# Attention projections of a two-block transformer kernel: three products of split operands in place of one float32 product

## The chip, the cores and the metric

The kernel runs on one core of a Trainium2 chip. The metric is the device time of one launch in microseconds (us), as the median of repeated runs. TensorE (PE, with its weight loads as PEld), VectorE (DVE), ScalarE (ACT), GpSimd (POOL) and SyncE (SP, which here only issues DMAs) run their own instruction streams and meet at semaphores.

## The reference, cut to what matters

Two transformer blocks run one after the other. The change is in the first one's mixer, attention with a forget gate, over 1024 tokens of width 1024 with 16 heads of 64 columns:

```python
def fox_mixer(x, w_in, b_f, w_out):
    proj = x @ w_in                      # [1024, 3 * 1024 + 16]
    q, k, v, f_logit = jnp.split(proj, [D_MODEL, 2 * D_MODEL, 3 * D_MODEL], axis=-1)
    ...
    log_f = jax.nn.log_sigmoid(f_logit.astype(jnp.float32) + b_f)
    c = jnp.cumsum(log_f, axis=1).transpose(0, 2, 1)
    ...
    s = jnp.einsum('bhqd,bhkd->bhqk', qi, k) * scale + cqi[..., None] - c[:, :, None, :]
    s = jnp.where(kpos[None, :] <= qpos[:, None], s, -jnp.inf)
    pr = jax.nn.softmax(s, axis=-1)
    o = jnp.einsum('bhqk,bhkd->bhqd', pr, v)
    return o @ w_out
```

Layer norm, a gated feed-forward network, and a second block (retention, a gated delta rule, a mixture of experts) follow. They are untouched.

## The kernel before, in words

**Stages.** The first stage is `stage_attention` (L127). The output projection, the FFN and the second block follow, each stage a block of its own that starts when the one before has ended.

**Pairs and units.** The attention stage works on pairs of heads (8 pairs p of 128 columns) and in each on 8 units t, one per 128 query rows; u = 8p + t. A unit t has t + 1 key blocks for each of the two heads. On PE a unit is, in this order (the loop after L357): `scores(u)`, `weigh(u-2)` (probabilities times v), one piece of projection work, `turn_first(u-1)` (128x128 transposes of the probabilities, the first 8), a second piece, `turn_second(u-1)` (the other transposes), the remaining pieces. In units 3 and 7 both first pieces stand ahead of `turn_first`. DVE does the row maxima, the output copy of u-2, the normalisation of both heads and the copies of the first transposes (`row_max`, `output`, `normalize`, `turned_copy`, L384 to L414). ACT does both exponentials, then the copies of finished pieces (`fill_copy`, L468) and of the second transposes (`turned_copy`, L500), in that order; in units 0 and 4 the copies of pieces come last.

**The projections.** q, k and v of a pair are made in six groups of four pieces (`V_LOW, Q_HIGH, K_HIGH, V_HIGH, Q_LOW, K_LOW`, L123), spread over the units by `PIECE_FROM` (L124); `LOW` and `HIGH` are the two halves of the tokens, `Q_LOW` and `K_LOW` are already for the next pair. All groups use the same PSUM bank 7: the first piece of a group waits until ACT has copied out the group before (`fill_out`). A q or k piece is two products of 128x128 weights (stationary) with 128x512 of x transposed (moving), in float32. A v piece is eight products of 128x128 of x with 128x128 of weights, in float32, and gives v with the tokens on the partitions. In the trace each float32 product is two MATMUL records. `scores(u)` of a wide unit waits for the exponentials of u-1, and from t = 4 on for the copy of K_HIGH.

**The weights.** `wqk` and `wv` are double buffered; SP loads a pair's weights once the products that read the buffer have ended (L233 to L241), two pairs ahead, and then loads the output projection's weights. GpSimd does nothing in the stage but issue one DMA.

**The start.** The first pair's q and k (both halves) are made up front in banks 0 to 3, k chunk by k chunk (L343 on). After chunk 3 PE does the forget gate's 64 thin products (f_bank), after chunk 5 one product that carries the sums over the tiles (L357). DVE makes the gate's cumulative sum in three bfloat16 parts (to L447), and SP spreads these with 24 small DMAs (L230). The first `scores` waits for all 24.

## Time and profile before

| | us |
|---|---|
| median of three runs | 3608.33 (3604.4 to 3608.97) |
| the profiled execution's own time | 3608.7 |
| its span on the core | 3606.9 |
| PE busy | 3174.3 (88%), 14928 matmul records |
| DVE, ACT, POOL busy | 1521.3 (42%), 1085.0 (30%), 1054.8 (29%) |

The span is what lies between the first and the last instruction of the core. Busy time is a union of instructions; a matmul's record is longer than the time to the next one's start, since matmuls overlap in the array. The rate of PE is therefore read from start to start. The granted clock is a share of full speed (1.00 is 2.4 GHz, 0.50 is 1.2 GHz).

### The profile page before, as it was taken

What the parts mean: (1) busy time and instruction counts of PE and PEld (TensorE: products, weight loads), DVE (VectorE), ACT (ScalarE), POOL (GpSimd) and SP (SyncE); (2) the same over time, 40 slices, a digit from 0 to 9 for tenths busy, and PEclk for the clock granted to TensorE, in tenths of its full rate; (3) what the DMA queues carried; (4) which work ended last, traced back from release to release, by engine and by line L of the source; (5) the groups of instructions that cost most, each with busy time, mean ns of one, the idle gap of its engine ahead of it and who ended that gap; (6) DMA issues with size and microseconds to landing.
All of it is one profiled execution on the core that took longest, in us unless ns stands there. A gap on an engine that the chain in (4) does not pass through costs nothing. (4 is left out here: it accounts for less than half of the span.)

```text
span 3606.9 us, 40987 instructions
## 1 busy us (share of the span) xinstructions
PE 3174.3 (88%) x14928; PEld 2220.4 (62%) x14928; DVE 1521.3 (42%) x2003; ACT 1085.0 (30%) x1457; POOL 1054.8 (29%) x539
## 2 busy tenths in 40 slices
PE   7999999979999979949699897999595799999993
PEld 4656566448888868834344444999542577777772
DVE  2443444431111111145520334444513778787875
ACT  1222222111111112210120122222202477777773
POOL 0000000123333324420000212222000378787774
PEclk9999999989999989969899998999797799999996
DMA  2000010211111132225510103100123699999995
GB/s 106 18 18 19 18 65 1 82 47 47 47 47 47 47 116 93 99 116 175 188 48 0 40 30 121 73 13 1 47 83 120 216 364 372 368 369 370 370 372 217
DMA packets 115216, 450.08 MB, mean 125 GB/s; under 512 B 14481, under 2 KB 15441, under 8 KB 109089
## 3 DMA queue, kind: packets, MB, share of 16 engines
q1 hardware_dynamic: 102066, 401.03, 30.1%
q0 software_dynamic: 7856, 28.64, 2.4%
q10 hardware_dynamic: 5184, 18.88, 1.3%
q8 instruction: 77, 1.26, 0.1%
q14 instruction: 33, 0.27, 0.0%
HBM read 404.30 MB, written 44.10 MB: 124 GB/s over the span
## 5 line engine op out<-in xcount | busy, mean ns | idle before, releaser
L2601 DVE TENSOR_TENSOR moe_w_low<-moe_raw_up,moe_w_high 128x1024 fp32r<-128x1024 f32 x288 | 436.4, 1553 | 156.5 <-ACT moe_w_high L2541 156.5
L2464 POOL TENSOR_TENSOR moe_w_low<-moe_raw_down,moe_w_high 128x1024 fp32r<-128x1024 f32 x144 | 417.3, 2928 | 148.4 <-ACT moe_w_high L2551 148.4
L2541 ACT ACTIVATE moe_w_high<-moe_raw_up 128x1024 fp32r<-128x1024 f32 x288 | 304.6, 1061 | 188.1 <-PE ps L2504 110.4
L91 PE MATMUL ps<-x1T_high,w_up_high 128*128 128x512 f32 x704 | 278.7, 396 | 13.7 <-POOL w_up_low L737 13.7
L91 PE MATMUL ps<-x1T_low,w_up_high 128*128 128x512 f32 x704 | 281.8, 400 | 0.0
L91 PE MATMUL ps<-x1T_high,w_up_low 128*128 128x512 f32 x704 | 276.9, 393 | 0.0
L585 POOL TENSOR_TENSOR res<-res,ln_b 128x1024 f32<-128x1024 f32 x16 | 37.5, 2346 | 780.3 <-DVE res L577 780.3
L253 PE MATMUL ps<-x0T,wqk 128*128 128x512 f32 x512 | 241.7, 608 | 10.3 <-DMA x0T<-in_xT 8.5
L2519 PE MATMUL ps<-moe_w_high,moe_x_high 128*128 128x512 f32 x576 | 229.4, 398 | 4.2 <-DVE moe_x_low L2632 4.2
L2521 PE MATMUL ps<-moe_w_high,moe_x_low 128*128 128x512 f32 x576 | 225.9, 392 | 0.0
L2520 PE MATMUL ps<-moe_w_low,moe_x_high 128*128 128x512 f32 x576 | 225.8, 392 | 0.0
L391 DVE TENSOR_REDUCE top<-ps 128x1 f32<-128x256 f32 (+7 forms) x128 | 91.0, 753 | 262.8 <-PE ps L298 262.8
L735 POOL TENSOR_TENSOR w_up_high<-w_up,consts 128x1024 fp32r<-128x1024 f32 x44 | 83.4, 1896 | 300.7 <-PE ps L91 289.3
L80 PE MATMUL ps<-xT,w_cols 128*128 128x512 f32 x384 | 171.2, 599 | 0.0
L497 ACT ACTIVATE probs<-ps,top 128x256 f32<-128x256 f32 (+7 forms) x128 | 93.9, 738 | 255.3 <-DVE top L391 255.3
L80 PE MATMUL ps<-w_rows,xT 128*128 128x512 f32 x384 | 165.5, 593 | 0.0
L91 PEld LDWEIGHTS ps<-x1T_high,w_up_high 128*128 128x128 f32 x704 | 132.8, 189 | 48.6 <-POOL w_up_low L737 14.1
L91 PE MATMUL ps<-w_down_high,h_high 128*128 128x512 f32 x352 | 137.8, 391 | 23.9 <-POOL w_down_low L873 22.6
L2551 ACT ACTIVATE moe_w_high<-moe_raw_down 128x1024 fp32r<-128x1024 f32 x144 | 147.2, 1055 | 35.2 <-DVE xT L2621 25.8
L873 POOL TENSOR_TENSOR w_down_low<-w_down,w_down_high 128x1024 fp32r<-128x1024 f32 x44 | 105.7, 2403 | 170.6 <-ACT w_down_high L857 170.6
L2504 PE MATMUL ps<-moe_w_high,moe_hid_high 128*128 128x512 f32 x288 | 101.5, 434 | 60.4 <-POOL moe_w_low L2464 60.4
L253 PEld LDWEIGHTS ps<-x0T,wqk 128*128 128x128 f32 x512 | 91.0, 191 | 101.8 <-issue 98.1
(417 smaller groups left out, 5918.4 us busy)
## 6 DMA issues: line engine op xcount, KB each, us to landing
moe_raw_up<-in_w SPq DMA_DIRECT2D x288, 512.0 KB, 10.3
moe_raw_down<-in_w SPq DMA_DIRECT2D x144, 512.0 KB, 7.3
w_ada<-in_w_ada SPq DMA_DIRECT2D x48, 512.0 KB, 4.7
w_up<-in_ffn_w_up SPq DMA_DIRECT2D x22, 1024.0 KB, 4.8
w_down<-in_ffn_w_down SPq DMA_DIRECT2D x44, 512.0 KB, 3.4
y_rows<-xT ACTq DMA_DIRECT2D x36, 512.0 KB, 8.2
wqk<-in_attn_wqk SPq DMA_DIRECT2D x8, 1024.0 KB, 4.9
y_rows<-zero_rows SPq DMA_DIRECT2D x1, 8192.0 KB, 29.2
```

The source lines that it names most:

```text
L80: ins = pe.matmul(out, stationary, moving, start=(n == 0), stop=(n == last))
L91: ins = pe.matmul(out, stationary, moving, start=start and n == 0, stop=stop and n == last)
L253: return pe.matmul(ps[:, bank, :], wqk[:, p % 2, k, j * P:(j + 1) * P], m.xT[:, k, h * HALF:(h + 1) * HALF], start=(k == 0), stop=(k == DT ...
L873: pool.tensor_tensor(w_low[:, s], w[:, s], w_high[:, s].bitcast(F32), ALU.subtract).then_inc(w_split[s], 1)
L2464: pool.tensor_tensor(w_low[:, down_slot(k)], raw_down[:, k], w_high[:, down_slot(k)].bitcast(F32), ALU.subtract).then_inc(down_low, 1)
L2504: ins = pe.matmul(ps[:, 5 + n, :], h[:, k, :], w[:, n * HALF:(n + 1) * HALF], start=first, stop=last)
L2519: pe.matmul(ps[:, 2 + j, :], x_high[:, k, :], high, start=first and a == 0, stop=False)
L2520: pe.matmul(ps[:, 2 + j, :], x_high[:, k, :], low, start=False, stop=False)
L2521: ins = pe.matmul(ps[:, 2 + j, :], x_low[:, k, :], high, start=False, stop=last and a == 1)
L2541: act.activation(w_high[:, up_slot(n)], raw_up[:, n], ACT.Copy).then_inc(up_high, 1)
L2551: act.activation(w_high[:, down_slot(k)], raw_down[:, k], ACT.Copy).then_inc(down_high, 1)
L2601: dve.tensor_tensor(w_low[:, up_slot(n)], raw_up[:, n], w_high[:, up_slot(n)].bitcast(F32), ALU.subtract).then_inc(up_low, 1)
```

## The change

x transposed and each pair's weights are split in a high part, which ACT writes as float32r (a Copy), and a low part, the difference, also float32r. Each product becomes three matmuls: high by high, high weights by low x, low weights by high x. v is made like q and k, with the weights stationary: its 128x512 result is v transposed. ACT copies it to `vT`, and a new piece of four 128x128 transposes (`VT_LOW`, `VT_HIGH`), which ACT copies out again, turns it. So there are eight groups of 4, 1, 4, 4, 4, 1, 4, 4 pieces. A q, k or v piece is now 6 matmuls of 128x512; a VT piece is 4 transposes. The units get 4, 4, 3, 2, 4, 4, 3, 2 pieces (before: 4, 3, 3, 2, 4, 3, 3, 2).

Weights are kept in three slots (v, q, k), raised by ACT at the end of units 3 (q), 4 (k) and 6 (v) for the next pair and lowered by GpSimd. One raw buffer serves all three: SP loads the next tensor when GpSimd has lowered the one before. At the start the first pair's q weights and all of x are lowered by DVE, its k and v weights by GpSimd. The thin products use the raw x. The product with the carries moves from after chunk 5 to after chunk 6. The output projection's weights are loaded after the last pair's V_HIGH, as their place holds the low x until then. The 24 spreading DMAs come in another order. The diff, cut:

```diff
-PIECES = 4
-V_LOW, Q_HIGH, K_HIGH, V_HIGH, Q_LOW, K_LOW = range(6)
-PIECE_FROM = (0, 4, 7, 10, 12, 16, 19, 22, 24)
+V_LOW, VT_LOW, Q_HIGH, K_HIGH, V_HIGH, VT_HIGH, Q_LOW, K_LOW = range(8)
+GROUP_SIZE = (4, 1, 4, 4, 4, 1, 4, 4)
+GROUP_AT = (0,) + tuple(itertools.accumulate(GROUP_SIZE))
+PIECE_GROUP = [g for g, n in enumerate(GROUP_SIZE) for _ in range(n)]
+PIECE_FROM = (0, 4, 8, 11, 13, 17, 21, 24, 26)
+V, Q, K = range(3)
...
-        wqk = sb("wqk", [P, 2, DT, 2 * P])
-        wv = sb("wv", [P, 2, DT, P])
-        wf = sb("wf", [P, DT, THIN])
+        x_high, x_low = sb("x0T_high", [P, DT, T], F32R), m.x_low
+        w_raw = sb("qkv_raw", [P, DT, P])
+        w_high, w_low = sb("qkv_high", [P, 3, DT, P], F32R), sb("qkv_low", [P, 3, DT, P], F32R)
+        vT = sb("vT", [P, HALF])
...
+        x_raw = [probs[:, k // 2, k % 2, :] for k in range(4)]
+        x_raw += [probsT[:, k // 2, 8 * (k % 2):8 * (k % 2) + 8, :].rearrange("p k n -> p (k n)") for k in range(4)]
+        first_raw = [None, v[:, 0], v[:, 1]]
+        wf = vT[:, 0:DT * THIN].rearrange("p (k n) -> p k n", n=THIN)
...
+        def wait_slot_free(eng, s, of):
+
+            if s == V:
+                eng.wait_ge(filled, through(of - 1, V_HIGH))
+            elif of == 1:
+                eng.wait_ge(qk_bank, 4)
+            else:
+                eng.wait_ge(filled, through(of - 1, Q_HIGH if s == Q else K_HIGH))
...
+            sp.dma_start(first_raw[Q], d["attn_w"][0, Q]).then_inc(first_loaded[Q], 16)
+            sp.dma_start(x_raw[0], d["xT"][:, 0, :]).then_inc(x_loaded[0], 16)
+            sp.dma_start(first_raw[K], d["attn_w"][0, K]).then_inc(first_loaded[K], 16)
+            for k in range(1, DT):
+                sp.dma_start(x_raw[k], d["xT"][:, k, :]).then_inc(x_loaded[k], 16)
             sp.dma_start(wf[:], d["attn_wf"]).then_inc(f_loaded, 16)
-            sp.dma_start(wqk[:, 0], d["attn_wqk"][0]).then_inc(wqk_loaded[0], 16)
-            for k in range(DT):
-                sp.dma_start(m.xT[:, k, :], d["xT"][:, k, :]).then_inc(x_loaded[k], 16)
             sp.dma_start(bf[:], d["attn_bf"]).then_inc(f_loaded, 16)
-            sp.dma_start(carries[:], d["fg_carries"]).then_inc(f_loaded, 16)
-            sp.dma_start(wv[:, 0], d["attn_wv"][0]).then_inc(wv_loaded[0], 16)
-            sp.dma_start(wqk[:, 1], d["attn_wqk"][1]).then_inc(wqk_loaded[1], 16)
-            sp.dma_start(wv[:, 1], d["attn_wv"][1]).then_inc(wv_loaded[1], 16)
+            sp.dma_start(carries, d["fg_carries"]).then_inc(f_loaded, 16)
+            sp.dma_start(w_raw[:], d["attn_w"][0, V]).then_inc(w_loaded, 16)
...
+            for p in range(1, PAIRS):
+                for s, before in ((Q, V), (K, Q), (V, K)):
+
+                    sp.wait_ge(lowered[before], p + (s != Q))
+                    sp.dma_start(w_raw[:], d["attn_w"][p, s]).then_inc(w_loaded, 16)
+
+            sp.wait_ge(filled, through(PAIRS - 1, V_HIGH))
...
+            def lower(s, of, raw):
+                pool.wait_ge(raised[s], of + 1)
+                pool.tensor_tensor(w_low[:, s], raw, w_high[:, s].bitcast(F32), ALU.subtract
+                                   ).then_inc(lowered[s], 1)
+
+            lower(K, 0, first_raw[K])
+            lower(V, 0, w_raw[:])
+            for p in range(1, PAIRS):
+                for s in (Q, K, V):
+                    lower(s, p, w_raw[:])
...
-            def qk_product(p, j, h, k, bank):
-                return pe.matmul(ps[:, bank, :], wqk[:, p % 2, k, j * P:(j + 1) * P],
-                                 m.xT[:, k, h * HALF:(h + 1) * HALF], start=(k == 0), stop=(k == DT - 1))
+            def product(s, h, k, bank):
+
+                cols = slice(h * HALF, (h + 1) * HALF)
+                pe.matmul(ps[:, bank, :], w_high[:, s, k, :], x_high[:, k, cols], start=(k == 0), stop=False)
+                pe.matmul(ps[:, bank, :], w_high[:, s, k, :], x_low[:, k, cols], start=False, stop=False)
+                return pe.matmul(ps[:, bank, :], w_low[:, s, k, :], x_high[:, k, cols], start=False,
+                                 stop=(k == DT - 1))
             def piece(u, n):
-                p, g, quarter = u // TT, n // PIECES, n % PIECES
-                if quarter == 0:
+                p, g = u // TT, PIECE_GROUP[n]
+                part = n - GROUP_AT[g]
+                if part == 0:
                     pe.wait_ge(fill_out, through(p, g) - 1)
-                if g in (V_LOW, V_HIGH):
-                    t = 4 * (g == V_HIGH) + quarter
-                    pe.wait_ge(wv_loaded[p % 2], 16 * (p // 2 + 1))
-                    ins = group(pe, ps[:, 7, quarter * P:(quarter + 1) * P],
-                                [(m.xT[:, k, t * P:(t + 1) * P], wv[:, p % 2, k, :]) for k in range(DT)])
+                if g in (VT_LOW, VT_HIGH):
+                    for i in range(4):
+                        ins = pe.transpose(ps[:, 7, i * P:(i + 1) * P], vT[:, i * P:(i + 1) * P], m.ident[:])
                 else:
-                    of, j, h = qk_of(p, g)
-                    pe.wait_ge(wqk_loaded[of % 2], 16 * (of // 2 + 1))
-                    for k in (2 * quarter, 2 * quarter + 1):
-                        ins = qk_product(of, j, h, k, 7)
-                if quarter == PIECES - 1:
+                    of, j, h = (p, -1, int(g == V_HIGH)) if g in (V_LOW, V_HIGH) else qk_of(p, g)
+                    pe.wait_ge(lowered[1 + j], of + 1)
+                    for k in (2 * part, 2 * part + 1):
+                        ins = product(1 + j, h, k, 7)
+                if part == GROUP_SIZE[g] - 1:
...
-            pe.wait_ge(wqk_loaded[0], 16)
+            pe.wait_ge(lowered[Q], 1)
             for k in range(DT):
-                pe.wait_ge(x_loaded[k], 16)
+                pe.wait_ge(x_lowered, k + 1)
                 for g in range(4):
-                    ins = qk_product(0, g % 2, g // 2, k, g)
+                    if g == 1:
+                        pe.wait_ge(lowered[K], 1)
+                    ins = product(1 + g % 2, g // 2, k, g)
                     if k == DT - 1:
                         ins.then_inc(qk_bank, 1)
                 if k == 3:
                     pe.wait_ge(f_loaded, 48)
-                    for n in range(4, DT):
+                    for n in range(DT):
                         pe.wait_ge(x_loaded[n], 16)
-                    thin_group(pe, ps[:, 7, 0:FCHUNK], wf, m.xT, TILES).then_inc(f_bank, 1)
-                if k == 5:
+                    for n in range(DT):
+                        for c in range(TILES):
+                            ins = pe.matmul(ps[c * THIN:(c + 1) * THIN, 7, 0:FCHUNK], wf[:, n, :],
+                                            x_raw[n][:, c * FCHUNK:(c + 1) * FCHUNK],
+                                            start=(n == 0), stop=(n == DT - 1))
+                    ins.then_inc(f_bank, 1)
+                if k == 6:
...
+            dve.wait_ge(raised[Q], 1)
+            dve.tensor_tensor(w_low[:, Q], first_raw[Q], w_high[:, Q].bitcast(F32), ALU.subtract
+                              ).then_inc(lowered[Q], 1)
+            for k in range(DT):
+                dve.wait_ge(x_raised, k + 1)
+                dve.tensor_tensor(x_low[:, k, :], x_raw[k], x_high[:, k, :].bitcast(F32), ALU.subtract
+                                  ).then_inc(x_lowered, 1)
...
+                    act.activation(vT[:], ps[:, 7, :], ACT.Copy).then_inc(fill_out, 1)
+                elif g in (VT_LOW, VT_HIGH):
+                    t = 4 * (g == VT_HIGH)
...
+            def raise_weights(s, of):
+                act.wait_ge(w_loaded, 16 * (raw_order(s, of) + 1))
+                if of:
+                    wait_slot_free(act, s, of)
+                act.activation(w_high[:, s], w_raw[:], ACT.Copy).then_inc(raised[s], 1)
+
+            def raise_first(s):
+                act.wait_ge(first_loaded[s], 16)
+                act.activation(w_high[:, s], first_raw[s], ACT.Copy).then_inc(raised[s], 1)
+
+            raise_first(Q)
+            for k in range(DT):
+                act.wait_ge(x_loaded[k], 16)
+                act.activation(x_high[:, k, :], x_raw[k], ACT.Copy).then_inc(x_raised, 1)
+                if k == 0:
+                    raise_first(K)
+            raise_weights(V, 0)
...
+                if p + 1 < PAIRS and t in (3, 4, 6):
+                    raise_weights({3: Q, 4: K, 6: V}[t], p + 1)
...
+        with ExitStack() as s2:
+            m.x_low = sb(s2, "x0T_low", [P, DT, T], F32R)
```

## Rows read from the trace of the kernel before

**Rows 1.** Busy time by stretch: engines, then PE clock, DMA share.

```profile
core 0: us, PE busy (x) PEld busy (x) DVE busy (x) ACT busy (x) POOL busy (x), PEclk, DMA share, GB/s
...
42.00:55.00 13.00, 0.11 (x1) 0.00 (x0) 0.00 (x0) 1.88 (x2) 0.00 (x0) 0.67 0.03 6
55.00:60.00 5.00, 4.80 (x25) 4.49 (x26) 1.29 (x6) 0.81 (x4) 0.00 (x0) 0.50 0.58 210
...
85.00:358.00 273.00, 270.76 (x1775) 168.08 (x1775) 113.18 (x246) 68.61 (x157) 0.00 (x0) 1.00 0.06 20
...
630.00:640.00 10.00, 8.43 (x60) 3.98 (x60) 5.75 (x12) 3.02 (x6) 0.00 (x0) 1.00 0.01 2
```

**Rows 2.** Timeline of SyncE's queue, issues in two neighbouring pairs.

```profile
227.23 0.33 SPq L238 DMA_DIRECT2D wqk<-in_attn_wqk  x1
...
304.10 0.33 SPq L238 DMA_DIRECT2D wqk<-in_attn_wqk  x1
```

**Rows 3.** Timeline of one pair, TensorE: start us, us, line, tiles.

```profile
371.42 3.70 PE L253 MATMUL ps<-x0T,wqk 128*128 128x512 f32 x8 [0.25 <-ACT qk L465]
...
386.49 1.04 PE L308 MATMUL ps<-consts,probs 128*128 128x128 f32 x8
387.37 5.52 PE L80 MATMUL ps<-wv,x0T 128*128 128x128 f32 x48
392.82 1.13 PE L291 MATMUL ps<-qk 64*128 64x512 f32 x4
...
396.29 1.98 PE L253 MATMUL ps<-x0T,wqk 128*128 128x512 f32 x4
...
406.69 1.98 PE L253 MATMUL ps<-x0T,wqk 128*128 128x512 f32 x4
```

**Rows 4.** Timeline of the start, all engines.

```profile
7.72 0.23 DVE L420 CAST ident<-consts 128x128 bf16<-128x128 f32 x1 [7.72 <-DMA consts<-in_consts]
...
8.54 15.82 PE L253 MATMUL ps<-x0T,wqk 128*128 128x512 f32 x32 [8.54 <-DMA x0T<-in_xT]
...
27.89 7.13 PE L253 MATMUL ps<-x0T,wqk 128*128 128x512 f32 x16
...
34.86 0.28 PE L357 MATMUL ps<-within,fg_carries 128*128 128x1 f32 x2
...
37.54 16.48 SPq L230 DMA_DIRECT2D negc<-parts  x24
...
55.20 0.80 PE L291 MATMUL ps<-qk 64*128 64x128 f32 x4 [13.09 <-DMA negc<-parts]
```

**Rows 5.** Timeline, TensorE in the FFN, first and last of 57 matmuls.

```profile
819.77 0.40 PE L91 MATMUL ps<-x1T_low,w_up_high 128*128 128x512 f32 x1
...
832.84 0.39 PE L91 MATMUL ps<-x1T_high,w_up_high 128*128 128x512 f32 x1
```

**Rows 6.** Timeline of the pair of rows 3, ScalarE.

```profile
370.77 0.60 ACT L465 ACTIVATE qk<-ps 128x512 f32<-128x512 f32 x1 [0.46 <-PE ps L253]
...
398.04 0.20 ACT L497 ACTIVATION_READ_ACCUMULATOR probs<-ps,top 128x1 f32 x1
...
408.71 0.60 ACT L465 ACTIVATE qk<-ps 128x512 f32<-128x512 f32 x1
```

**Rows 7.** Page, costliest groups: raising and lowering 128x1024 tiles elsewhere.

```profile
L2601 DVE TENSOR_TENSOR moe_w_low<-moe_raw_up,moe_w_high 128x1024 fp32r<-128x1024 f32 x288 | 436.4, 1553 | 156.5 <-ACT moe_w_high L2541 156.5
...
L2541 ACT ACTIVATE moe_w_high<-moe_raw_up 128x1024 fp32r<-128x1024 f32 x288 | 304.6, 1061 | 188.1 <-PE ps L2504 110.4
...
L873 POOL TENSOR_TENSOR w_down_low<-w_down,w_down_high 128x1024 fp32r<-128x1024 f32 x44 | 105.7, 2403 | 170.6 <-ACT w_down_high L857 170.6
```

**Rows 8.** DMA issues, 0 to 700 us: size, time to landing.

```profile
w_attn_out<-in_attn_w_out SPq DMA_DIRECT2D x2, 2048.0 KB, 10.3
```

**Rows 9.** Groups by form, 60 to 660 us: the widest normalisation.

```profile
L402 DVE TENSOR_SCALAR probs<-probs,inv 128x1024 f32<-128x1024 f32 x16 | 12.1, 754 | 0.6
```

**Rows 10.** Timeline of the last pair, TensorE, a unit without pieces.

```profile
636.44 0.66 PE L308 MATMUL ps<-consts,probs 128*128 128x128 f32 x4 [1.57 <-DVE probsT L411]
```

More of the change, by code:

```diff
@@ L203, in pieces @@
             p, t = u // TT, u % TT
-            return [n for n in range(PIECE_FROM[t], PIECE_FROM[t + 1]) if not skipped(p, n // PIECES)]
+            return [n for n in range(PIECE_FROM[t], PIECE_FROM[t + 1]) if not skipped(p, PIECE_GROUP[n])]
         def through(p, g):
-            return 6 * p + g + 1 - 2 * (p > 0 or g > K_HIGH)
+            return 8 * p + g + 1 - 2 * (p > 0 or g > K_HIGH)
         def qk_of(p, g):
@@ L328, in weigh @@
                 p, t = u // TT, u % TT
-                pe.wait_ge(fill_out, through(p, V_HIGH if t >= 4 else V_LOW))
+                pe.wait_ge(fill_out, through(p, VT_HIGH if t >= 4 else VT_LOW))
                 pe.wait_ge(first_out, firsts[u + 1])
@@ L351, in _ @@
                     pe.wait_ge(f_loaded, 48)
-                    for n in range(4, DT):
+                    for n in range(DT):
                         pe.wait_ge(x_loaded[n], 16)
-                    thin_group(pe, ps[:, 7, 0:FCHUNK], wf, m.xT, TILES).then_inc(f_bank, 1)
-                if k == 5:
+                    for n in range(DT):
+                        for c in range(TILES):
+                            ins = pe.matmul(ps[c * THIN:(c + 1) * THIN, 7, 0:FCHUNK], wf[:, n, :],
[3 more added lines that the diff above has]
+                if k == 6:
                     pe.wait_ge(f_step, 5)
-                    pe.matmul(ps[:, 6, 0:1], carries[:], within[:, FCHUNK - 1:FCHUNK], start=True, stop=True
+                    pe.matmul(ps[:, 6, 0:1], carries, within[:, FCHUNK - 1:FCHUNK], start=True, stop=True
                               ).then_inc(carried, 1)
@@ L517, in _ @@
             for u in range(UNITS):
-                ends = [n for n in pieces(u) if n % PIECES == PIECES - 1]
+                p, t = u // TT, u % TT
+                ends = [n for n in pieces(u) if n + 1 in GROUP_AT]
                 late = u % TT in (0, 4)
```

74 lines of the change are left out of this document (32 added, 42 removed).

## The prediction

> **What bounds the kernel now.** I first read the busy time by stretch, to see what the attention stage waits for. Over the middle pairs PE is busy 270.76 of 273 us at clock 1.00, DVE 113.18, ACT 68.61 and POOL 0 [rows 1]: PE is the bound and three engines have room. The DMA queue's timeline gives the length of a pair, 304.10 - 227.23 = 76.87 us [rows 2]. The timeline of PE through a pair shows hardly a hole; the one short wait is 0.25 us, for ACT's copy out of bank 7 [rows 3]. So time that PE saves in a pair is saved in the end, as far as what the pieces cover (row maxima, exponentials, copies) does not come out from under them. The start is another regime: PE stands idle about 13 us until the spreading DMAs of the gate have landed, and the chain to them is carries product at 34.86, issues from 37.54, scores at 55.20 [rows 4]. There, only what moves the carries product counts.
>
> **The products.** A float32 q or k group is 8 products of 512 columns. 16 records took 27.89 to 34.86, 6.97 us [rows 4]; I leave some 0.1 of it to the change-over at the end, which stays, so 6.87. The new matmul exists elsewhere, in the FFN: 57 starts from 819.77 to 832.84 are 0.2334 us apart, with a weight load for each and the clock full [rows 5]. A group of 24 costs 5.60, so a q or k group saves 1.27. A v group is 64 records; 48 of them took 387.37 to 392.82, 5.45 us [rows 3], so 7.27 in all; against 5.60 it saves 1.67. The new turning piece has four transposes; eight took 386.49 to 387.37, 0.11 each [rows 3], so it costs 0.44. Per middle pair, then: 4 x 1.27 + 2 x 1.67 - 2 x 0.44 = 7.5 us.
>
> **The new waits.** The turning piece is a group of its own in the one bank 7. The next piece waits until ACT has copied it out, and ACT does its exponentials first, so ahead of that copy a whole row maximum and exponential stand. I follow each unit with the times of rows 3 and 6.
> - Unit 5: the projection work starts at 396.29. Four transposes to 396.73, `turn_first` (8 x 0.11) to 397.61. ACT's last exponential ends at 398.04 + 0.20 = 398.24 [rows 6], the copy takes 0.60, PE sees it 0.05 later, as it does after the copy at 370.77 (end 371.37, PE at 371.42 [rows 3, 6]): 398.89. The wait is 1.3; the change-over of 0.1 is in it: 1.2. Queued behind it on PE are three q pieces, `turn_second` and the scores of unit 6; DVE and ACT wait for those.
> - Unit 6: piece at 406.69, now 1.40 and a change-over to 408.19, `turn_first` to 409.07. ACT's copy can't start before 408.71, as now [rows 6], and ends at 409.31: PE goes on at 409.36. Wait 0.3. It is hidden now, by the longer piece.
> - Unit 1: exponentials are short there. The transposes drain for about 0.17 (a record of 1.04 is followed by the next start after 0.88 [rows 3]), the copy is 0.60, the wake-up 0.05, and two transposes of 0.22 cover: 0.6. I take 0.5.
> - Unit 2's wait of 0.25 stays: piece and copy move up together. The other boundaries have a whole `scores` and `weigh` between them.
> Together 2.0 per pair, so a middle pair saves 7.5 - 2.0 = 5.5 us and lasts 71.3.
>
> **The pairs in sum.** Six middle pairs: 33.0. Pair 0 has two v groups and the next pair's two q/k groups: 3.3 + 2.5 - 0.44 (the other turning piece stands in a stretch that waits for the softmax chain) - 1.5 for units 5 and 6 = 3.9. Pair 7: 3.3 + 2.5 - 0.44 - 0.5 = 4.9; its units 5 to 7 have no pieces and already wait for DVE 1.57 us [rows 10], which covers the turning piece. Sum 41.8.
>
> **Raising and lowering.** Per pair ACT gets 3 raisings of 1.06 [rows 7] and 2 more copies of 0.60, 4.4 us on an engine busy a quarter of the time; they are queued after a unit's last copy, and the next exponential waits for a `scores` and a row maximum, over 3 us in the wide units, so I cost them at nothing; without that cover at 1.06 each, 22 us. The second path is raise, lower (POOL, 2.40 [rows 7]), load 0.5 MB. The load is under the 10.3 us that 2 MB took [rows 8]. Three rounds of under 14 us fit in 71. Q is raised at the end of unit 3 and used in unit 5, K at 4 and 6, v at 6 and in the next pair: a unit of some 9 us (71.3 / 8) lies between. On SP the loads stand behind the 24 spreading DMAs once, and behind nothing later. The output projection's weights now start at the end of the last pair's unit 4, with three units and the tail of the stage left; at 76.87 / 8 = 9.6 us a unit, less without pieces, that is over 20 us as an estimate, and two overlapping loads of 10.3 [rows 8] fit.
>
> Does the lowering hold up DVE? The widest normalisation takes 754 ns for 1024 elements, while a subtraction of two tiles as wide takes 1553 on the same engine [rows 7, 9], so DVE has a fast form for it. The Trainium skill (SBUF — State Buffer, Who interferes with whom) says that such a form, or one with two SBUF inputs, and a GpSimd operation shut each other out for a whole instruction; no row of this stage has both. By place there is no meeting: q's lowering would run about 1.1 to 3.5 us into unit 4, k's 1.8 to 4.2 into unit 5, while unit 5's last exponential ends 398.24 - 392.82 = 5.4 into the unit [rows 3, 6] and the normalisation comes near there. I take nothing in the pairs; the upper end is a rival.
>
> **The start.** PE began at 8.54 [rows 4]. Now DVE must first finish the small casts (from 7.72 [rows 4], some 0.5), then lower q's weights and chunk 0 of x; alone I put each at 1.4 (1.55 where GpSimd works too [rows 7]). So PE starts at about 11.0. Up to the carries product it has 7 chunks of 12 matmuls (19.6), the 3.5 of the thin products (24.36 to 27.89) and some 2 us of half clock, as now (the first 32 records took 15.8 where their later pace gives 13.8 [rows 4]): 36.1. k's weights, 2.4 us on POOL after a raising, are ready about 0.5 later than PE asks for them. If POOL's lowering gets ahead of DVE's chunk 0 it is 2.4 more. Against 34.86 this is 1.8 to 4 us later; I take 2.5. Nothing gains: the spreading and its 24 issues stay, and the first scores with them.
>
> **Sum.** 41.8 - 2.5 = 39.3 us. From the profiled execution, 3608.7 (span 3606.9 and 1.8 around it), that is 3569.4; the median is 0.4 lower, so 3569. Later stages load nothing in other order, and I cost them at zero.
>
> **Rivals.**
> - **The waits stay hidden** (ACT is free earlier than in the old rows, since the scores come sooner after the last copy): 6 x 2.0 + 1.5 + 0.5 = 14 less, 3555. Against: both terms of unit 5's wait are read straight from ACT. Chance 0.09.
> - **The chain comes out further.** The shorter pieces uncover more: the scores waiting for the exponentials, `turn_second` for DVE's copies as in the last pair, or ACT's raisings in front of an exponential. Another 1.5 us per pair in seven pairs: 3580. Chance 0.14.
> - **The clock.** Between 42 and 55 us PE was idle, and the next 5 us had clock 0.50 [rows 1]; but in 630 to 640, with waits of 1.57, it was 1.00 [rows 1, 10]. Were two stretches of 3.5 us in each of seven pairs at half clock, each would cost 1.75: 24.5 us, 3594. The Trainium skill (TensorE: Matmul & The Clock Gate, A second HAM failure mode: psum-queue depth-cycling) has a kernel whose small idle times between groups did this, and the one bank 7 is such a queue. The last pair speaks against. Chance 0.06.
> - **Slower: GpSimd's lowering shuts DVE out.** Place: `normalize` of units 4, 5 and 7, with PE's transposes behind it. If each of 3 x 7 lowerings delays PE by its whole 2.40: 50.4 us, 3620. It passes 3609 once each costs over 39.3 / 21 = 1.9. For it: POOL goes from 0 to 7.2 us per pair. Against: the places above, and that most of DVE's work in a unit reads PSUM. Chance 0.04.
> - **It doesn't do what it says:** the three matmuls are no faster than the one float32 product here (another operand or weight-load limit) and the time is within 7 us of before. Against: the same form at 0.2334 in the FFN. Chance 0.02.
> - The forecast: 0.65, by itself 3560 to 3578 (the start 1.8 to 4, unit 5's wait 0.8 to 2 in seven pairs, the groups' savings 10% off).
>
> **Range and chances.** 3555 to 3584 takes in the first two rivals and leaves out the last three. 0.2% is about 7 us, what a measurement of this kernel can tell from no change. Faster 0.94 (forecast, the first three rivals), same 0.02, slower 0.04.
>
> **What would show it.** In the changed trace: SP issues of neighbouring pairs 71.3 apart; matmuls of `ps<-w_high,x_high` 0.23 apart; PE waiting for ACT's copy of vT's transposes 1.2 us in unit 5 and about 0.5 in unit 1; first `scores` near 57.7; the stage's end some 39 us earlier; DVE's means in the stage as before. The prediction is wrong if PE's clock falls in the stage, if DVE's normalisations get longer, or if ACT stands at a raising for a load.

## The result, and the profile after

| | before | changed |
|---|---|---|
| median, us | 3606.62 (3604.4 to 3608.97, 4 runs) | 3561.06 (3559.79 to 3562.18, 4 runs) |
| profiled execution, span | 3606.9 | 3557.7 |
| first load of the next stage (end of attention) | 653.98 | 613.01 |
| what follows to the end of the span | 2952.9 | 2944.7 |

The ratio is 0.9873, 95% interval 0.9861 to 0.9886. Run again beside other kernels, the same code gave 0.9888 (0.9873 to 0.9903), experiment e11. The forecast was 3569 (3555 to 3584).

Where the time went is read first from the stage's end. These are the first loads of the next stage, in the timeline of SyncE's queue before and after:

```profile
653.98 0.33 SPq L610 DMA_DIRECT2D res<-in_x  x1
```

```profile
613.01 0.33 SPq L680 DMA_DIRECT2D res<-in_x  x1
```

653.98 - 613.01 = 41.0 us; the forecast for the stage was 39.3. The other 8 us between the two profiled spans are behind the stage, where nothing was changed. Over all thirteen profiles of this study (the kernels before and changed, and the eleven experiments, which all share that rest) it took between 2944.7 and 2953.5. One place of this scatter is seen in the timelines of TensorE in the mixing stage, the same 256 records before and after:

```profile
2617.59 113.04 PE L80 MATMUL ps<-qkv,xT 128*128 128x512 f32 x256 [2.80 <-DMA qkv<-in_w_mix_out]
```

```profile
2574.80 110.13 PE L80 MATMUL ps<-qkv,xT 128*128 128x512 f32 x256 [1.87 <-DMA qkv<-in_w_mix_out]
```

They start 42.8 us apart and end 45.7 apart, 2.9 us more: in the 25 us around their start PE's granted clock was 0.77 in the one (2605 to 2630) and 0.92 in the other (2562 to 2587). The other 5 us are not placed. So the two executions that were profiled lie 8 us apart behind the stage, and the 41 us at the stage's end are read as the change; e11 comes back to this.

**Through the pairs.** Busy time by stretch of the changed kernel, beside [rows 1] (columns as there):

```profile
core 0: us, PE busy (x) PEld busy (x) DVE busy (x) ACT busy (x) POOL busy (x), PEclk, DMA share, GB/s
...
42.00:55.00 13.00, 0.00 (x0) 0.00 (x0) 0.00 (x0) 0.00 (x0) 0.00 (x0) 0.57 0.03 6
55.00:60.00 5.00, 3.31 (x13) 2.59 (x14) 1.30 (x6) 0.81 (x4) 0.00 (x0) 0.50 0.34 107
...
85.00:355.00 270.00, 261.46 (x1742) 182.84 (x1738) 118.44 (x263) 85.00 (x184) 26.63 (x11) 1.00 0.07 22
```

PE is now busy 261.46 of 270 us, where it was 270.76 of 273. It has real holes, and the clock stays at 1.00. The timeline of POOL gives the length of a pair, as SP's queue did in [rows 2], since it lowers q's weights once per pair:

```profile
359.85 2.65 POOL L272 TENSOR_TENSOR qkv_low<-qkv_raw,qkv_high 128x1024 fp32r<-128x1024 f32 x1 [39.48 <-ACT qkv_high L564]
...
431.16 2.65 POOL L272 TENSOR_TENSOR qkv_low<-qkv_raw,qkv_high 128x1024 fp32r<-128x1024 f32 x1 [39.51 <-ACT qkv_high L564]
```

71.31 us; before 76.87, forecast 71.3. The holes, in TensorE's timeline of one pair (units 5, 6 and 1), beside [rows 3]:

```profile
371.92 0.66 PE L300 MATMUL ps<-consts,vT 128*128 128x128 f32 x4
372.42 1.04 PE L342 MATMUL ps<-consts,probs 128*128 128x128 f32 x8
374.41 0.50 PE L286 MATMUL ps<-x0T_high,qkv_high 128*128 128x512 f32 x1 [0.96 <-ACT v L527]
...
384.44 1.04 PE L342 MATMUL ps<-consts,probs 128*128 128x128 f32 x8
385.55 0.50 PE L286 MATMUL ps<-x0T_high,qkv_high 128*128 128x512 f32 x1
...
411.61 0.66 PE L300 MATMUL ps<-consts,vT 128*128 128x128 f32 x4
412.10 0.38 PE L342 MATMUL ps<-consts,probs 128*128 128x128 f32 x2
412.95 0.50 PE L286 MATMUL ps<-x0T_high,qkv_high 128*128 128x512 f32 x1 [0.47 <-ACT v L527]
```

The turning piece at 371.92 takes 0.50, `turn_first` at 372.42 follows, and then PE waits 0.96 us for ACT's copy of the turned v (L527). The same in unit 1: 0.47 before 412.95. Before 385.55 there is a hole of 0.24, counted otherwise: at its pace of 0.11 per transpose `turn_first`, from 384.44, would have let the next start at 385.31. Counted so, unit 5's hole is 1.1. ScalarE's timeline of the same units shows why, beside [rows 6]:

```profile
373.68 0.20 ACT L547 ACTIVATION_READ_ACCUMULATOR probs<-ps,top 128x1 f32 x1
373.77 0.59 ACT L527 ACTIVATE v<-ps 128x512 f32<-128x512 f32 x1
...
384.91 0.59 ACT L513 ACTIVATE qk<-ps 128x512 f32<-128x512 f32 x1
...
412.30 0.60 ACT L527 ACTIVATE v<-ps 128x512 f32<-128x512 f32 x1 [1.00 <-PE ps L300]
```

In unit 5 the copy at 373.77 follows the exponential's end directly: ACT was busy, and the piece had long been ready. The same in unit 6 at 384.91, behind an exponential that ends at 384.82 + 0.09. In unit 1, at 412.30, ACT had waited for PE: there the wait is only the copy's own 0.60.

**The start.** TensorE's timeline, beside [rows 4]:

```profile
9.82 0.77 PE L286 MATMUL ps<-x0T_high,qkv_high 128*128 128x512 f32 x1 [9.82 <-DVE x0T_low L469]
...
11.95 0.79 PE L286 MATMUL ps<-x0T_high,qkv_high 128*128 128x512 f32 x1 [0.51 <-POOL qkv_low L272]
...
36.34 0.28 PE L398 MATMUL ps<-qk 128*128 128x1 f32 x2
...
56.69 0.80 PE L325 MATMUL ps<-qk 64*128 64x128 f32 x4 [17.22 <-DMA negc<-parts]
```

PE starts at 9.82 and not at 8.54, has to wait 0.51 for k's low weights from POOL, reaches the carries' product at 36.34 (34.86 before) and the first scores at 56.69 (55.20). So the start costs 1.5 us in this execution.

### The profile page after: what moved, and what is told of

Same layout as the page of the kernel before. It is cut to its first block and busy times, and to the rows that moved or that the text cites. A ratio compares the mean times of both kernels' runs of the same rounds, so it can differ in the third digit from the quotient of the medians.

```text
span 3557.7 us, 40458 instructions
## 1 busy us (share of the span) xinstructions
PE 3116.4 (88%) x14608; PEld 2227.6 (63%) x14608; DVE 1536.4 (43%) x2012; ACT 1124.6 (32%) x1505; POOL 1114.3 (31%) x562
## 5 line engine op out<-in xcount | busy, mean ns | idle before, releaser
L272 POOL TENSOR_TENSOR qkv_low<-qkv_raw,qkv_high 128x1024 fp32r<-128x1024 f32 x22 | 53.5, 2434 | 468.8 <-ACT qkv_high L564 468.8
L286 PE MATMUL ps<-x0T_high,qkv_high 128*128 128x512 f32 x384 | 163.9, 427 | 22.5 <-ACT v L527 10.0
L91 PEld LDWEIGHTS ps<-x1T_high,w_up_high 128*128 128x128 f32 x704 | 132.5, 188 | 45.7 <-POOL w_up_low L807 14.2
L91 PE MATMUL ps<-w_down_high,h_high 128*128 128x512 f32 x352 | 138.1, 392 | 23.8 <-POOL w_down_low L943 22.5
L2621 ACT ACTIVATE moe_w_high<-moe_raw_down 128x1024 fp32r<-128x1024 f32 x144 | 147.2, 1056 | 33.4 <-DVE xT L2691 29.5
L91 PEld LDWEIGHTS ps<-x1T_low,w_up_high 128*128 128x128 f32 x704 | 132.5, 188 | 34.6
```

The lines of the kernel that those rows point to most:

```text
L91: ins = pe.matmul(out, stationary, moving, start=start and n == 0, stop=stop and n == last)
L286: pe.matmul(ps[:, bank, :], w_high[:, s, k, :], x_high[:, k, cols], start=(k == 0), stop=False)
L2621: act.activation(w_high[:, down_slot(k)], raw_down[:, k], ACT.Copy).then_inc(down_high, 1)
```

## The experiments

Lengths of pairs are read from POOL's timeline, as above. Where a run was made once, its verdict is read from the attention stage of its profile; its time in the table has the scatter of the rest. Pairs repeat within 0.1 us, but the stage's end is not that sharp: the changed kernel's own code gave 613.01 and 614.26 (e11). Two places of this scatter show. In the start the first matmuls stand 0.43 apart, and how long they do differs: to 16.4 in the changed kernel, to 14.7 in e4 and e8, to 18.0 in e11. In the stage's last unit the 16 transposes and the waits between them take 2.6 us in nine of the thirteen profiles and 3.3 to 3.6 in e1, e2, e4 and e7, at a granted clock of 0.66 in place of 1.00; so the stages of these four end some 1 us late.

| | pair, us | first scores | stage's end | time, us |
|---|---|---|---|---|
| before | 76.87 | 55.20 | 653.98 | 3606.62 |
| changed | 71.31 | 56.69 | 613.01 | 3561.06 |
| e1 no turning | 68.59 | 57.23 | 595.63 | 3547.13 |
| e2 float32 in the pieces | 79.05 | 56.90 | 670.76 | 3624.54 |
| e3 turned v between | 70.38 | 56.70 | 606.52 | 3560.03 |
| e4 carries after chunk 5 | 71.26 | 53.27 | 611.13 | 3561.51 |
| e5 POOL twice | 71.37 | 56.32 | 612.81 | 3568.47 |
| e6 DVE lowers | 71.32 | 56.37 | 612.44 | 3567.81 |
| e7 two products | 60.96 | 56.97 | 538.25 | 3488.91 |
| e8 early gate | 71.31 | 47.79 | 604.26 | 3555.11 |
| e9 two queues | 71.31 | 50.50 | 606.52 | 3556.3 |
| e10 three parts | 70.43 | 42.28 | 592.26 | 3542.15 |
| e11 changed again | 71.32 | 57.64 | 614.26 | 3565.98 |

### e1: no turning of v

```diff
-GROUP_SIZE = (4, 1, 4, 4, 4, 1, 4, 4)
-PIECE_FROM = (0, 4, 8, 11, 13, 17, 21, 24, 26)
+GROUP_SIZE = (4, 4, 4, 4, 4, 4)
+PIECE_FROM = (0, 4, 7, 10, 12, 16, 19, 22, 24)
...
                 if g in (V_LOW, V_HIGH):
-                    act.activation(vT[:], ps[:, 7, :], ACT.Copy).then_inc(fill_out, 1)
-                elif g in (VT_LOW, VT_HIGH):
-                    t = 4 * (g == VT_HIGH)
+                    t = 4 * (g == V_HIGH)
                     act.activation(v[:, p % 2, t:t + 4, :]..., ps[:, 7, :], ACT.Copy).then_inc(fill_out, 1)
```

> Leaves out the turning of v: the two turning groups and their copies are gone, the schedule of units is the one of before, and v is copied out as it is (transposed, so the result is another). Theory (turning costs its transposes plus the waits for ACT's copy): per middle pair 2 x 0.49 for the transposes, 0.96 in unit 5 and 0.47 in unit 1, together 2.4 us; neighbouring pairs 68.9 us apart where the changed kernel has 71.3, and about 18 us less in all, 3543. Rival (the waits are only moved: the softmax chain then shows at the same places): 1 us per pair, 3553.

POOL's timeline:

```profile
418.14 2.65 POOL L272 TENSOR_TENSOR qkv_low<-qkv_raw,qkv_high 128x1024 fp32r<-128x1024 f32 x1 [38.40 <-ACT qkv_high L559]
...
486.73 2.65 POOL L272 TENSOR_TENSOR qkv_low<-qkv_raw,qkv_high 128x1024 fp32r<-128x1024 f32 x1 [38.39 <-ACT qkv_high L559]
```

68.59 us per pair, 2.72 less than the changed kernel (2.4 expected); the stage ends 17.4 us sooner (some 18.5 but for the slow last unit); the ratio to the kernel before is 0.9841 (0.9823 to 0.9859). No wait for the copy of v is left in its waits. So turning v costs its transposes and its two waits, 2.4 us by the rows above, and 0.3 more that I put down to the change-overs around them without a row for it; the softmax chain did not take its place.

### e2: one float32 product in the pieces

```diff
-                        ins = product(1 + j, h, k, 7)
+                        ins = pe.matmul(ps[:, 7, :], w_high[:, 1 + j, k, :].bitcast(F32),
+                                        x_high[:, k, h * HALF:(h + 1) * HALF].bitcast(F32),
+                                        start=(k == 0), stop=(k == DT - 1))
```

> The pieces of q, k and v use one float32 product of the high parts in place of the three float32r matmuls (the low parts are left out there); the start, raising, lowering, turning and all waits stay as in the changed kernel. Theory (PE bound; what the split saves is the products): a group goes from 24 x 0.23 = 5.5 to 6.87 us, six groups per pair give 8.2, less the 0.25 wait of unit 6 that is covered again: pairs 79.2 us apart, the stage about 61 us longer than the changed kernel's, 3622, above the kernel before by what turning, its waits and the start cost. Rival (the gain comes from v being made like q and k, not from the three products): under 30 us longer.

TensorE's timeline:

```profile
386.90 3.70 PE L305 MATMUL ps<-x0T_high,qkv_high 128*128 128x512 f32 x8
390.44 0.82 PE L344 MATMUL ps<-consts,probs 128*128 128x128 f32 x6
...
408.17 1.98 PE L305 MATMUL ps<-x0T_high,qkv_high 128*128 128x512 f32 x4 [0.96 <-ACT v L529]
...
450.42 5.42 PE L305 MATMUL ps<-x0T_high,qkv_high 128*128 128x512 f32 x12 [0.47 <-ACT v L529]
```

A pair takes 79.05 (79.2 expected), the stage is 57.7 us longer than the changed one's: 6 x 7.74 = 46.4 in the middle pairs, the rest in the first and the last, which have four groups each and not six. 61 were expected, with 1.37 us per group. Two pieces take 386.90 to 390.44, 3.54 us, against 2.87 in the changed kernel, so a group saves 1.34, and six of them less the 0.24 of unit 6, which the longer piece covers here, give the 7.74 to 0.1. The waits of units 5 and 1 are where they were, 0.96 and 0.47, though the pieces are longer: no piece stands ahead of them. Against the kernel before this one is slower, ratio 1.0063 (1.0042 to 1.0084), 16.8 us at the stage's end. That is the price of the new structure without its product: turning (17.4 by e1) and the start (1.5), less what v gains by 512 columns in one product; that difference, 2 us as it stands and nearly 5 without the slow last unit of e1 and e2, is read from no row of its own.

### e3: the turned v between the exponentials

```diff
                 exponent(u, 0)
+                if t == 5:
+                    fill_copy(u, ends[0])
+                    ends = ends[1:]
                 exponent(u, 1)
```

> In unit 5 ACT copies the turned v between its two exponentials, not behind them. Theory (PE's wait of 0.96 in unit 5 is ACT's order): the wait falls to about 0.1, pairs 70.4 us apart, the stage 7 us shorter. Rival (the second exponential, 0.6 later, delays the next scores or DVE's normalisation and gives it back): pairs stay at 71.3.

The waits, 60 to 614 us (us in total, times, longest):

```profile
PE ps L286 <- ACT v L527: 3.3, 7, 0.5
```

Pairs of 70.38, as expected, and the stage ends 6.5 us sooner. Of PE's waits for the copy of v, 10.0 us in 14 times, 3.3 in 7 remain: unit 1's. The wait of unit 5 was ACT's order of work. Its single time, 3560.03, shows nothing of this, 6.5 us being inside the scatter of a single run.

### e7: two products

```diff
-                        ins = product(1 + j, h, k, 7)
+                        pe.matmul(ps[:, 7, :], w_high[:, 1 + j, k, :], x_high[:, k, cols], start=(k == 0),
+                                  stop=False)
+                        ins = pe.matmul(ps[:, 7, :], w_low[:, 1 + j, k, :], x_high[:, k, cols], start=False,
+                                        stop=(k == DT - 1))
```

> Leaves out the middle product (high weights by low x) in the pieces, so a piece is 4 matmuls. Theory (PE is still the bound after the change, but its cover is thin): a group costs 3.7 in place of 5.5, 6 x 1.85 = 11.1 us per pair if nothing came out from under it; the waits for ACT's copies and DVE's turned tiles grow in units 2, 5, 6 and 7 by some 0.4 each, so pairs at about 62. Rival (the softmax chain is already next): pairs over 66.

The waits, 60 to 614 us (us in total, times, longest):

```profile
PE ps L306 <- ACT v L531: 10.0, 14, 1.0
...
PE ps L306 <- ACT qk L517: 7.0, 14, 0.5
```

60.96 per pair, where about 62 were expected: 10.35 less, of 11.1 at most. The waits for copies of v are unchanged and those for copies of q and k went from 1.8 to 7.0 us over the stage. The chain of maxima and exponentials is not the next bound: another third of the products could go and nine tenths of it would come out at the end.

### e5 and e6: GpSimd twice, and DVE in its place

```diff
                 pool.wait_ge(raised[s], of + 1)
+                if of:
+                    pool.tensor_tensor(spare[:], raw, w_high[:, s].bitcast(F32), ALU.subtract)
```

> GpSimd does each lowering of the pairs from the second on twice, the first time into a spare tile. Theory (GpSimd is covered and its places miss DVE's normalisations, apart from short overlaps): POOL's work doubles to 14 us per pair, DVE's normalisations grow by at most one overlap per pair (about 1 us, not on PE's path), pairs stay at 71.3 us. Rival (GpSimd shuts DVE out and PE pays): pairs get several us longer.

DVE's and POOL's timelines around unit 4:

```profile
362.80 2.07 DVE L446 TENSOR_SCALAR probs<-probs,inv 128x640 f32<-128x640 f32 x1
364.78 1.27 DVE L455 COPY probsT<-ps 128x512 f32<-128x512 f32 x2
```

```profile
359.50 2.65 POOL L274 TENSOR_TENSOR spare<-qkv_raw,qkv_high 128x1024 fp32r<-128x1024 f32 x1 [37.15 <-ACT qkv_high L567]
362.12 2.39 POOL L275 TENSOR_TENSOR qkv_low<-qkv_raw,qkv_high 128x1024 fp32r<-128x1024 f32 x1
```

This is the lock in plain view: a normalisation of 640 columns, 554 ns otherwise, starts at 362.80 and takes 2.07 us; POOL's second lowering starts at 362.12 and takes 2.39, to 364.51. It ends at 364.87, 0.36 behind the lowering, so part of its own 0.55 was done under it. The mean of this form over the stage is 1131 ns, that of 768 columns 1247 in place of 621: 2.8 us more of normalisation per pair, where at most 1 was expected. The pair nevertheless takes 71.37. What stands behind the normalisation, the copies of turned tiles, is needed by PE only later: its waits for them are 7.0 us in 11 times over the stage, as in the changed kernel. So one half of the rival was right, GpSimd and DVE do shut each other out, and the other half wrong, PE did not pay.

```diff
                 normalize(u, 1)
+                if p + 1 < PAIRS and t in (4, 5, 7):
+                    s = {4: Q, 5: K, 7: V}[t]
+                    dve.wait_ge(raised[s], p + 2)
+                    dve.tensor_tensor(w_low[:, s], w_raw[:], w_high[:, s].bitcast(F32), ALU.subtract
+                                      ).then_inc(lowered[s], 1)
```

> DVE does the lowerings of the pairs from the second on, one unit later than GpSimd did, at the end of its work in units 4, 5 and 7. Theory (DVE has room, 40% busy): 3 x 1.2 us more on DVE per pair, pairs at 71.3 to 72. Rival (GpSimd is needed, since DVE's chain sets the copies that PE waits for): 2 us or more per pair.

DVE's timeline:

```profile
398.45 1.22 DVE L506 TENSOR_TENSOR qkv_low<-qkv_raw,qkv_high 128x1024 fp32r<-128x1024 f32 x1
399.58 0.48 DVE L428 TENSOR_REDUCE top<-ps 128x1 f32<-128x128 f32 x2
```

DVE lowers in 1.22 us (POOL in 2.34 to 2.65). The lowering shown is that of v's weights behind unit 7; it is done just when the row maxima of unit 0 follow, at 399.58. Pairs of 71.32, nothing lost, though ACT now stands 1.39 us at the raising of k's weights (441.33), whose load waits for q's lowering: GpSimd is not needed for this. With GpSimd idle in the pairs the 512-column normalisations have a mean of 487 ns, as before the change; in the changed kernel and in e5 it is 617:

```profile
L439 DVE TENSOR_SCALAR probs<-probs,inv 128x512 f32<-128x512 f32 x16 | 7.8, 487 | 0.6
```

Both kernels have longer times (3568.47, 3567.81) than the changed one had; the kernel before took 3613.08 on that chip, and their rests behind the stage, 2953.1 and 2953.5, are the two longest.

### e4, e8 and e9: the start

e4 lets the carries' product follow chunk 5, one chunk sooner:

```diff
-                if k == 6:
+                if k == 5:
                     pe.wait_ge(f_step, 5)
```

> The product with the carries goes back to after chunk 5. Theory (the start's end is set by that product through DVE's parts and the 24 DMAs): it runs at about 33.6 where it ran at 36.3, and the first scores come at 54.0 where they came at 56.7; 2.7 us less. Rival (the gate's sum is not ready then, or the DMAs' landing is set by something else): under 1 us.

TensorE's timeline:

```profile
32.93 0.28 PE L398 MATMUL ps<-qk 128*128 128x1 f32 x2
...
53.27 0.80 PE L325 MATMUL ps<-qk 64*128 64x128 f32 x4 [14.50 <-DMA negc<-parts]
```

The product runs at 32.93, 3.4 us sooner than at 36.34, and the first scores come 3.4 sooner. 2.7 of it are the chunk's 12 matmuls; the other 0.7 is there before the moved product: the first matmuls stood 0.43 apart only to 14.7 and not to 16.4, and the thin products began at 23.76 and not at 24.45. That is scatter of the start: in e11, which is the changed kernel's own code, they began at 25.41 and the first scores came at 57.64. The granted clock of the rows is 1.00 in all of these, so what holds the pace at 0.43 is open. The stage ends only 1.9 sooner. The windows behind the first scores, of e4 and of the changed kernel, and those of the tail of e4's stage:

```profile
53.00:57.00 4.00, 3.73 (x14) 2.92 (x15) 1.30 (x6) 0.81 (x4) 0.00 (x0) 0.50 0.39 131
57.00:61.00 4.00, 4.00 (x14) 3.14 (x13) 0.00 (x0) 0.00 (x0) 0.00 (x0) 0.72 0.00 0
```

```profile
57.00:60.00 3.00, 3.00 (x13) 2.25 (x12) 1.30 (x6) 0.81 (x4) 0.00 (x0) 0.50 0.38 147
60.00:62.00 2.00, 2.00 (x8) 1.60 (x7) 0.00 (x0) 0.00 (x0) 0.00 (x0) 0.80 0.00 0
```

```profile
601.00:604.00 3.00, 2.32 (x11) 1.78 (x12) 1.42 (x2) 0.87 (x2) 0.00 (x0) 0.66 0.01 3
604.00:606.00 2.00, 2.00 (x14) 1.69 (x16) 0.69 (x1) 0.87 (x2) 0.00 (x0) 0.66 0.04 8
```

In e4 PE stays at half clock longer: it is 0.50 to 57 and 0.72 from there to 61, in the changed kernel 0.50 to 60 and 0.80 to 62. From the first scores that is some 6 us at low clock against 4, and POOL's first lowering behind it comes 71.92 to 74.48, only 2.6 sooner. In pair 6 the lead is 2.8 still (529.10 against 531.94). The last us of it goes in the tail, where e4's clock was 0.66 from 601 to 606 and the changed kernel's 1.00 over the same work, from 604 to 607.5. That code is the same in all these kernels, and the fall is there in four of the thirteen profiles, so I take it for scatter. The longer half clock at the start does not belong to an earlier start as such: e8 kept 8.7 of its 8.9 us to POOL's first lowering (65.78 against 74.48).

e8 moves both products earlier (`k == 3` to 1 for the thin ones, `k == 6` to 3 for the carries), e9 shares the spreading DMAs between SP and ACT:

> The gate's thin products go from after chunk 3 to after chunk 1 and the product with the carries from after chunk 6 to after chunk 3. Theory (the start's end is that product plus some 20.3 us of parts, 24 DMAs and landing): all of x is there by about 17.6, the thin products run from 19 to 22.6, the carries' product at 28.1, the first scores at 48.5 where they came at 56.7; 8.2 us less. Rival: the thin products wait for the last chunk of x or DVE is late with the gate's sum, under 5 us less.

TensorE's timeline:

```profile
47.79 0.80 PE L325 MATMUL ps<-qk 64*128 64x128 f32 x4 [9.06 <-DMA negc<-parts]
```

```diff
+            act.wait_ge(parted, 6)
+            for j in range(3):
+                for c in range(TILES):
+                    act.dma_start(negc[64 + j:64 + j + 1, :, c * FCHUNK:(c + 1) * FCHUNK],
+                                  parts[c * THIN + 1:c * THIN + HEADS:2, j, :]).then_inc(spread, 16)
             for g in range(4):
                 act.wait_ge(qk_bank, g + 1)
```

> 12 of the 24 spreading DMAs are issued by ACT, ahead of its copies of the first q and k. Theory (SP's issue, 0.69 us each, is what the 16.5 us are): both queues issue for 8.2 us, the first scores come 8 us sooner, near 48.5. Rival (landing or the DMA engines set it): under 3 us.

ScalarE's timeline of e9:

```profile
39.02 9.23 ACTq L585 DMA_DIRECT2D negc<-parts  x12
48.29 2.06 ACT L514 ACTIVATE qk<-ps 128x512 f32<-128x512 f32 x4 [16.66 <-issue]
```

e8: first scores at 47.79, 8.9 us sooner where 8.2 were expected, the stage's end 8.75 sooner; the 0.7 more is the start's scatter again, as in e4, since here too the slow pace ended at 14.7 and the carries' product ran at 27.44 in place of 28.1. e9: first scores at 50.50, 6.2 sooner where 8 were expected. Both queues issue 12 DMAs in some 9 us (8.85 on SP, 9.23 on ACT), so the issue was most of the 16.5. But ACT's copies of the first q and k stand behind its issues and end at 48.29 + 2.06 = 50.35, and PE's wait is now for them. I had named neither price nor place of this in the expectation.

### e10 and e11: three parts together, and the changed kernel again

e10 is e3, e8 and e9 in one. It was run beside e11, the changed kernel as it is.

> The changed kernel with the turned v copied between the exponentials of unit 5, the gate's products early (thin after chunk 1, carries after chunk 3) and the spreading on two queues. Theory (the parts add, until q and k set the start): 6.5 us from the pairs, the first scores near 41 where they came at 56.7, since PE ends the first q and k at 39.1 and ACT copies them, and no cold clock after it (another 1.8): about 24 us, the stage's end near 589, 3537. Rival (ACT's issues hold up its copies, or the parts overlap): under 15 us.

TensorE's timeline, and the windows around the first scores:

```profile
28.02 0.28 PE L399 MATMUL ps<-qk 128*128 128x1 f32 x2
...
42.28 0.49 PE L326 MATMUL ps<-qk 64*128 64x128 f32 x4 [2.98 <-ACT qk L514]
```

```profile
39.00:42.30 3.30, 0.32 (x4) 0.05 (x2) 0.00 (x0) 2.21 (x5) 0.00 (x0) 1.00 0.28 78
42.30:46.60 4.30, 4.30 (x17) 3.34 (x18) 1.29 (x6) 1.94 (x5) 0.00 (x0) 0.62 0.17 68
```

> The changed kernel as it is, on the same chip as the one with the three parts. Theory: 41 us less than before in the attention stage, and whatever the rest of the program adds is scatter between runs: ratio near 0.9886, the stage's end at 613. Rival (the change also shortens later stages by 4 to 8 us): ratio near 0.987 again and a rest behind the stage of 2945 in the profile.

e10: median 3542.15 (3539.55 to 3545.91, 5 runs), ratio to the kernel before 0.9824 (0.9811 to 0.9838); the changed kernel beside it 3565.98 and 0.9888. So e10 is 23.8 us faster than the changed kernel by the medians and 614.26 - 592.26 = 22.0 at the stage's end, 24 having been expected: it is faster than the kernel before and than the changed one. The first scores come at 42.28, 1.3 later than expected, again behind ACT's copies. The idle time in front of them has shrunk to 2.98 us, but the clock still falls: 1.00 in the window to 42.3, and 0.62 in the one from there. The 1.8 us expected from a clock that stays up were not had.

e11: the stage's end 614.26 and the rest 2948.8. That agrees with the theory of scatter; the first pair of profiles had shown 8 us of it. Only one profile of the kernel before exists. The medians help: less the stage's end of the profile (653.98 for the kernel before), they leave for the rest 2951.5 (e1) and 2953.8 (e2) against 2950.0 of the kernel before beside them, 2949.9 (e10) and 2951.7 (e11) against 2952.0, and 2948.1 against 2952.6 in the first comparison. So the rest is longer in two, shorter in three, and no saving of 4 to 8 us behind the stage is shown.

## Why the prediction was right

It was right in its sign, its size and its main mechanism; point by point:

- **PE as the bound.** Held. A pair lost 5.56 us, forecast 5.5. e7 goes further: PE is still the bound after the change.
- **The products.** Held: in the pieces the new matmuls stand 0.23 apart, 12 of them taking 2.87 us from 355.16 to 358.03 in the changed kernel. e2 gives their worth alone: 7.74 us per middle pair, against 7.6 for six groups at the forecast's 1.27. Without them the change would have been a loss.
- **The turning piece.** Its transposes take 0.50, not 0.44. With its waits it costs 2.72 per pair by e1; the forecast had 0.88 + 1.7 = 2.6.
- **The waits.** Unit 5: 1.2 forecast, 0.96 measured; in the forecast's own count, from the end of `turn_first` at its pace (373.30) to the next start (374.41), 1.3 and 1.1. Unit 6: 0.3 and 0.24. Unit 1: 0.5 and 0.47. Unit 2: 0.25, as before. The cause in unit 5, the exponentials ahead of the copy, is shown by e3.
- **Raising and lowering at nothing.** Held in the time: 22.0 us on ACT, 51.2 on POOL over the stage. e5 and e6 bear out POOL's part; ACT's has no experiment of its own, but no raising of the changed kernel's pairs waited for a load, and the pairs came out as forecast without it. One step of the reasoning was wrong, and by the prediction's own list of signs (DVE's means as before; wrong if the normalisations get longer) it counts against it. Its argument from place put q's lowering 1.1 us into unit 4, which is where it is, ahead of unit 4's normalisation and free of any other; but unit 3's second normalisation runs just there (359.80 beside POOL's 359.85). The mean of the 512-column form rose from 486 to 617 ns; one execution of it in pair 0 makes up nearly all of that:

```profile
74.55 2.57 DVE L443 TENSOR_SCALAR probs<-probs,inv 128x512 f32<-128x512 f32 x1
```

```profile
74.48 2.35 POOL L272 TENSOR_TENSOR qkv_low<-qkv_raw,qkv_high 128x1024 fp32r<-128x1024 f32 x1 [52.23 <-ACT qkv_high L564]
```

  A normalisation of 0.49 us took 2.57, to 77.12, and POOL's lowering ran from 74.48 to 76.83. That agrees with the rule of the Trainium skill (SBUF — State Buffer, Who interferes with whom) that I had weighed: the one waits for the whole of the other. Which of them waits hangs on less than 0.1 us here: in pair 0 POOL started 0.07 ahead and DVE waited, in the six other pairs DVE started first (by 0.05 at 359.80), kept its 0.49, and POOL's lowering took 2.65 in place of 2.35. It cost PE nothing that can be seen, and that is cover and not absence of the meeting: the reason given (the places miss each other) failed, the price of nothing held because PE needs what stands behind the normalisation only later, as e5 shows.
- **The start.** Forecast 2.5 us, measured 1.5, and the two do not differ by one term. PE began at 9.82 and not at 11.0: DVE took 1.16 for q's weights and 1.21 for chunk 0, where I had put 1.4 each, and the constants landed at 6.97 and not 7.72. But from there to the carries' product PE took 26.5 us, where the forecast's terms give 25.6 (36.1 - 11.0, and the 0.5 for k's weights). More of the first matmuls at the pace of 0.43 make most of that; the forecast calls this half clock, while the rows grant 1.00 there, before and after. The forecast's terms alone come to 36.6 for the product, near the measured 36.34; the 2.5 held another 0.8 for the case that POOL's lowering of k's weights gets ahead of DVE's chunk 0. It did not: it took 2.95 beside DVE's, but came behind it. So part of this agreement is two errors that cancel, and a us of it is scatter (e11's first scores came at 57.64, 2.4 later than before).
- **The sum.** The stage gave 41.0 for 39.3: the pairs 42.5 for 41.8 (the six middle ones 33.4 for 33.0), the start 1.5 for 2.5. The medians' 45.6 (by the interval of the ratio 41 to 50) lie above it, e11's 40.0 (3606.02 - 3565.98) below; I put the difference down to scatter, on the grounds given at e11.
- **Rivals.** Hidden waits and float32r no faster than float32 are ruled out by the rows above. So is a falling clock: with waits of 0.96, 0.24 and 0.47 in each pair, all behind the one bank 7, it stayed at 1.00 from 85 to 580 us. The kernel that the Trainium skill tells of (TensorE: Matmul & The Clock Gate, A second HAM failure mode: psum-queue depth-cycling) lost its clock to small idle times between groups; this trace does not show that at these sizes. That kernel also cycles through banks where this one has a single bank 7, so the likeness that the prediction drew is loose, and the stretches of 3.5 us that it priced stand in no row. That the chain comes out further in the pairs is ruled out by their 71.31 us and by e7. GpSimd's lock exists; its price on PE's path was under 0.1 us per pair even at double load.

## What to carry to other kernels

Where an engine is busy 99% of a stretch, cost the filler work per piece from start-to-start times of the same instruction form elsewhere in the trace, and then follow each new hand-over on the engine that makes it: a copy queued behind a long operation costs what is left of that operation. A short piece that ends a group on a single PSUM bank is paid twice, by itself and by its copy. Where two engines can shut each other out, ask what waits behind the blocked operation and not only whether the places miss each other: a shift of 0.1 us changed here who waits. Judge a change of some 10 us in a program of 3600 by the end of its own stage, since the unchanged rest scattered by 9 us between profiles; and one of 1 us by the length of its pairs, since the stage's end scattered by 1.25.

## What the runs showed of the hardware

- DVE and GpSimd shut each other out: a 0.55 us normalisation became 2.07 behind a lowering (e5) and ended 0.36 after it, one of 0.49 became 2.57 and ended 0.29 after it (changed kernel, 74.55), and a lowering became 2.65 and not 2.35 where DVE had started 0.05 us before it. With GpSimd idle in the pairs (e6) the normalisations had their old 487 ns.
- float32r matmuls of 128x512 with a weight load for each came 0.227 us apart (changed kernel, 17.55 to 24.14) to 0.233 (the FFN of [rows 5]) at full clock; the float32 product of the same size takes two records 0.43 apart, so three of the one cost 0.8 of one of the other.
- An idle time of 2.98 us of PE was followed by a clock of 0.62 over the next 4.3 us (e10), while the waits of 0.96, 0.24 and 0.47 in each pair left it at 1.00. In the stage's last unit, behind the same waits of 1.66 and 0.67 us, it was 1.00 in nine of the thirteen profiles and 0.66 in four (e1, e2, e4, e7), where the same transposes took 0.7 to 1.0 us longer.
- In the start float32r matmuls stood 0.43 apart, to 14.7 us in two profiles, 16.4 in the changed kernel's and 18.0 in e11's, and then 0.23 apart, while the granted clock of the rows was 1.00 throughout.
- The small DMAs took 0.69 us each to issue on SP (24 in 16.47 us), and 12 on each of two queues ran side by side in 8.85 and 9.23 us (e9), 0.74 and 0.77 each.
